# Two transformer blocks on one core: layer parameters loaded in two lots, the first expert step reordered, vector work spread over the recurrence, and squares moved to ScalarE

## What is computed

```python
# block 1 (one layer)
h   = rms_norm(x, norm1_g)                 # w_in: gated linear attention (GLA) + 3 dilated attention groups
gla = gla_chunked(q, k, v, log_a)          # 4 heads of 128, chunks of 16
att = dilated attention, 4 heads, q and k rms-normalised per head of 128
x   = x + (sigmoid gates * (gla proj, att proj)) @ w_out
x   = x + hier_moe(...)                    # 4 groups x 8 experts, width 512, 2 experts per token in one group
# block 2 (two layers l = 0, 1)
z   = rms_norm(x) @ w_in_2[l]              # 2840 columns: spatial gating | RWKV-7 time mix | NSA attention
z_b = z_b + (shift(z_b) - z_b) * mu        # the shift by one token that needs the previous row
rwkv: state = state * w + (state . -kk) (kk * a) + v k, per token, 4 heads of 64
nsa : compressed, selected and windowed attention with rotated queries and keys
x   = x + concat(...) @ w_out_2[l]
x   = x + (l == 0: swiglu, width 2816 | l == 1: 8 experts of width 2816, 2 per token)
x   = x + (p[l] @ ple_proj) * sigmoid(rms_norm(x) @ ple_gate)
```

## Time and profile before

| | |
|---|---|
| runs | 2486.06, 2474.56, 2478.81 us; median 2478.81 |
| profiled execution | 2484.66 us, span of the core 2482.9 us, mean granted TensorE clock 0.963 |
| busy share | PE 94%, PEld 77%, DVE 74%, ACT 59%, POOL 2% |
| DMA | 617.61 MB, mean 249 GB/s |

### The profile page before, as it was taken

The page is one execution under the profiler, slowest core; times in us unless marked ns, Lnnn a source line. Parts: engine busy times, 40 slices in busy tenths (PEclk is TensorE's granted clock), DMA queues, the critical chain, the costliest instruction groups (busy, mean ns, idle before and its releaser), DMA issues.

```text
span 2482.9 us, 30596 instructions
## 1 busy us (share of the span) xinstructions
PE 2335.2 (94%) x12418; PEld 1901.3 (77%) x12418; DVE 1842.8 (74%) x1911; ACT 1469.8 (59%) x1438; POOL 39.1 (2%) x41
## 2 busy tenths in 40 slices
PE   7989988999999998788999998889999999999997
PEld 6878767888888886676788777668888877888885
DVE  5875657888898885676554567578888968888885
ACT  5344536776777774435444553466776756767764
POOL 0000000000000000020000002000000000000000
PEclk8999988999999998899999999889999999999999
DMA  9444445999999995505464551249999988999991
GB/s 234 128 119 136 152 144 206 363 367 355 370 356 370 355 370 168 164 3 178 153 202 165 167 163 53 81 178 364 355 366 359 357 306 301 363 361 358 367 343 52
DMA packets 281225, 617.61 MB, mean 249 GB/s; under 512 B 31848, under 2 KB 130408, under 8 KB 243696
## 3 DMA queue, kind: packets, MB, share of 16 engines
q1 hardware_dynamic: 279664, 611.33, 71.5%
q10 hardware_dynamic: 1408, 4.19, 0.4%
HBM read 612.34 MB, written 1.05 MB: 247 GB/s over the span
## 4 chain that ended last, share of the span: by engine, by line
PE 84%; DVE 9%; ACT 4%; issue 2%; DMA 1%; SPq 0%; DVEq 0%; ACTq 0%
PE ps L566 24%; PE ps L567 24%; PE ps L568 24%; DVE ring_parts L590 3%; ACT high_parts L586 2%; PE ps L2143 1%; PE ps L2782 1%; PE ps L2113 1%; PE ps L3063 1%; PE ps L2114 1%; PE ps L3076 1%; PE ps L2155 0%; PE ps L2154 0%; DMA arena<-arena 0%; DVE arena L1347 0%
## 5 line engine op out<-in xcount | busy, mean ns | idle before, releaser
L590 DVE TENSOR_TENSOR ring_parts<-ring,high_parts 128x2048 fp32r<-128x2048 f32 (+1 forms) x574 | 1282.9, 2274 | 177.4 <-ACT high_parts L586 171.0
L586 ACT CAST high_parts<-ring 128x2048 fp32r<-128x2048 f32 (+1 forms) x574 | 1079.5, 1897 | 194.4 <-PE ps L568 186.8
L568 PE MATMUL ps<-high_parts,arena_parts 128*128 128x512 f32 (+2 forms) x1560 | 621.0, 398 | 0.0
L566 PE MATMUL ps<-high_parts,hT_parts 128*128 128x512 f32 (+2 forms) x1120 | 459.3, 410 | 32.4 <-DVE ring_parts L590 13.7
L567 PE MATMUL ps<-ring_parts,hT_parts 128*128 128x512 f32 (+2 forms) x1120 | 447.8, 400 | 0.0
L566 PE MATMUL ps<-high_parts 128*128 128x512 f32 x912 | 365.2, 400 | 0.0
L567 PE MATMUL ps<-ring_parts,high_parts 128*128 128x512 f32 x912 | 359.3, 394 | 0.0
L568 PE MATMUL ps<-high_parts 128*128 128x512 f32 x912 | 356.5, 391 | 0.0
L568 PEld LDWEIGHTS ps<-high_parts,arena_parts 128*128 128x128 f32 x1560 | 300.6, 193 | 69.2
L566 PE MATMUL ps<-high_parts,arena_parts 128*128 128x512 f32 x744 | 294.9, 396 | 10.5 <-DVE ring_parts L590 4.7
L567 PE MATMUL ps<-ring_parts,arena_parts 128*128 128x512 f32 x744 | 294.1, 395 | 0.0
(11 more groups left out here) (531 smaller groups left out, 1837.8 us busy)
## 6 DMA issues: line engine op xcount, KB each, us to landing
ring<-in_moe_w SPq DMA_DIRECT2D x248, 1024.0 KB, 5.5
ring<-in_w_gate SPq DMA_DIRECT2D x64, 1024.0 KB, 6.0
ring<-in_w_up SPq DMA_DIRECT2D x64, 1024.0 KB, 5.8
ring<-in_w_down SPq DMA_DIRECT2D x64, 1024.0 KB, 5.8
ring<-in_w_in SPq DMA_DIRECT2D x104, 256.0 KB, 4.5
ring<-in_ffn_w SPq DMA_DIRECT2D x44, 512.0 KB, 5.0
ring<-in_w_in SPq DMA_DIRECT2D x20, 1024.0 KB, 5.1
ring<-in_moe_w SPq DMA_DIRECT2D x32, 512.0 KB, 5.0
```

What stands on the lines that cost most here:

```text
L566: pe.matmul(dst, a_hi, b_hi, start=first, stop=False, skip_group_check=True)
L568: return pe.matmul(dst, a_lo, b_hi, start=False, stop=last, skip_group_check=True)
L586: act.copy(high_flat(p), raw_flat(p)).then_inc(upper, 1)
L590: dve.tensor_tensor(raw_flat(p, ring_parts_flat), raw_flat(p), f32(high_flat(p)), ALU.subtract).then_inc(split, 1)
```

## The change

Five edits. (1) `load_layer` becomes `load_soon` (11 loads) and `load_later` (9 loads: the two layer-norm rows, the gating bias and weights, the position and compression weights). In layer 0 pieces 0 to 4 are streamed first, then the 11, pieces 5 to 8, the first shift, pieces 9 on, the second shift, and then the 9. In layer 1 both lots are issued in a row where all 20 stood. PE waits for the second lot after the first scores (slot 20), DVE in hook (10, 0). (2) Expert stages: in step 0 ACT also splits up piece 0 of step 1 and runs the silu ahead of the router's exponential, and DVE takes low parts of step 1's pieces 0 and 1 around the gate weights; in step 1 PE runs up piece 0, then the gates, up piece 1, then turns step 0's hidden part. For b = 4 the gates come after up piece 1 instead of after piece 3. `rows` on DVE comes before piece 1 instead of piece 2. (3) `masked` moves from ahead of level 1 to behind `rw_z1`. (4) Both key rotations at k = 1; the queries' rotation is cut: first product at k = 2, three at k = 3, the two sums in the loop over chunks. (5) ACT makes the dilated squares, right behind its evacuation of the block.

```diff
+        LATER = (8, 9, 10, 14, 15, 16, 17, 18, 19)
@@ SP, layer 0
-                    stream(sp, pieces[0:4])
+                    stream(sp, pieces[0:5])
                     sp.wait_ge(sig("xT_psum"), XT_AT["mix0"] + KC // 2)
-                    load_layer(sp, 0)
-                    stream(sp, pieces[4:10])
+                    load_soon(sp, 0)
+                    stream(sp, pieces[5:9])
...
                 shift_sp(sp, l, 0)
-                stream(sp, pieces[10:])
+                stream(sp, pieces[9:] if l == 0 else pieces[10:])
                 shift_sp(sp, l, 1)
+                if l == 0:
+                    load_later(sp, 0)
@@ first_act hook (phase 1) / dil_squares
+                    if i == 2 * keys_block(h):
+                        after_block(act, keys_block(h))
+                        if h == 0:
+                            act.wait_ge(sig("g_o"), 3)
+                        act.activation(d_sq[h], d_z[h % 2][:, 0:6]..., ACT.Square).then_inc(sig("d_rt"), 1)
-                vstep(dve, dve.tensor_tensor(d_sq[h], qk, qk, ALU.mult))
+                dve.wait_ge(sig("d_rt"), 2 * h + 1)
                 dve.tensor_reduce(d_ss, d_sq[h], AX, ALU.add).then_inc(sig("d_ms"), 1)
@@ moe_main_pe
-                if held:
+                if held and s > 1:
                     turn(held)
...
                 up(st, 0)
+                if s == 1:
+                    pe.wait_ge(*ended(f"{f.name}_gates"))
+                    gates(0)
...
                 up(st, 1)
+                if grouped and b:
+                    gates(b)
+                if s == 1:
+                    turn(held)
                 for h in range(2, len(st.up)):
...
-                if grouped:
-                    pe.wait_ge(*ended(f"{f.name}_gates"))
-                    gates(b)
@@ moe_main_act
+                    if s == 1 and h == 0:
+                        continue
                     split_high(act, p)
-                if st is f.plan[0]:
-                    router_exp_act(act, f)
-                if grouped:
+                    if s == 1 and h == 1:
+                        gate(0)
+                if s == 0:
+                    split_high(act, f.plan[1].up[0])
+                if grouped and b:
                     gate(b)
...
                 silu(st)
+                if s == 0:
+                    router_exp_act(act, f)
@@ moe_main_dve
-                    if grouped and h == 2:
+                    if grouped and h == 1:
                         rows(b)
+                    if s == 1 and h < 2:
+                        continue
...
+                if s == 0:
+                    split_low(dve, f.plan[1].up[0])
                     gates1_dve(dve) if f is moe1 else gates2_dve(dve)
+                    split_low(dve, f.plan[1].up[1])
@@ rwkv, DVE
-                dve.wait_ge(*at("rw_scores", 2))
-                ... six products, then rw_masked
                 for k in range(1, LEV):
                     ... rw_z{k}
+                    if k == 1:
+                        masked()
                     dve.wait_ge(*at(f"rw_dt{k}"))
...
                         ins.then_inc(sig(f"rw_H{n + 1}"), 1)
+                        if n == 0:
+                            dve_aside(dve, "queries")
@@ dve_aside
-                if k in (1, 2): one key rotation each
-                elif k == 3: rotate(dve, n_qr, z[:, :, CQ:CKC], CH)
+                if k == 1: both key rotations
+                elif k in (2, 3):
+                    rotate(dve, n_qr, z[:, :, CQ:CKC], CH, ((0,), (1, 2, 3))[k - 2])
+                elif k == "queries":
+                    rotate(dve, n_qr, z[:, :, CQ:CKC], CH, (4, 5)).then_inc(sig("nsa_rot"), 1)
```

More of the change, by code:

```diff
@@ L828, in layer_loads, with load_soon, load_later, loaded_later @@
             return lot
[L830 to L834, removed]
+        LATER = (8, 9, 10, 14, 15, 16, 17, 18, 19)
+        N_SOON = len(layer_loads(0)) - len(LATER)
+        def load_soon(eng, l):
+            for k, (dst, src) in enumerate(layer_loads(l)):
+                if k not in LATER:
+                    eng.dma_start(dst, src).then_inc(sig("layer_params"), 16)
+        def load_later(eng, l):
+            for k, (dst, src) in enumerate(layer_loads(l)):
+                if k in LATER:
+                    eng.dma_start(dst, src).then_inc(sig("params"), 16)
+        def loaded_later(l):
+            return sig("params"), 16 * (len(P1_LOADS) + len(LATER) * (l + 1))
         MI = Arena(arena)
@@ L1261, in hook @@
                 for h in range(DH):
+                    if i == 2 * keys_block(h):
+                        after_block(act, keys_block(h))
+                        if h == 0:
+                            act.wait_ge(sig("g_o"), 3)
+                        act.activation(d_sq[h], d_z[h % 2][:, 0:6].rearrange("p k t e -> p (k t) e"), ACT.Square)\
+                            .then_inc(sig("d_rt"), 1)
                     if i == D_TURN[h] // 2:
@@ L2188, in moe_main_pe @@
             held = None
-            for st in f.plan:
+            for s, st in enumerate(f.plan):
                 b = st.bucket
-                if held:
+                if held and s > 1:
                     turn(held)
@@ L2344, in moe_main_dve @@
             select(0)
+            assert f.plan[0].n == 512
             held, before = None, None
-            for st in f.plan:
+            for s, st in enumerate(f.plan):
                 b = st.bucket
@@ L2623, in pe_ @@
                     mm.then_inc(sig("rw_scores"), 1)
+                    pe.wait_ge(*loaded_later(l))
                     for h in range(AH):
@@ L2930, in dve_, with masked @@
                 dve.tensor_tensor(w_T, w_T, idn, ALU.add).then_inc(sig("rw_t1"), 1)
-                dve.wait_ge(*at("rw_scores", 2))
-                for k, (dst, m) in enumerate(((w_MT, tri_str_c), (w_RB, tri_inc_c), (w_RK, tri_inc_c))):
-                    for s in range(2):
-                        part = slice(s * NT * HP, (s + 1) * NT * HP)
-                        bank, col = ((1, 2), (1, 2), (3, 0))[k][s], (k % 2) * S
-                        ins = dve.tensor_tensor(dst[:, part, :], blocks(ps[:, bank, col:col + S]), wide(m[:], NT * HP), ALU.mult)
-                ins.then_inc(sig("rw_masked"), 1)
+                def masked():
+                    dve.wait_ge(*at("rw_scores", 2))
+                    for k, (dst, m) in enumerate(((w_MT, tri_str_c), (w_RB, tri_inc_c), (w_RK, tri_inc_c))):
+                        for s in range(2):
+                            part = slice(s * NT * HP, (s + 1) * NT * HP)
+                            bank, col = ((1, 2), (1, 2), (3, 0))[k][s], (k % 2) * S
+                            ins = dve.tensor_tensor(dst[:, part, :], blocks(ps[:, bank, col:col + S]), wide(m[:], NT * HP), ALU.mult)
+                    ins.then_inc(sig("rw_masked"), 1)
                 def bonus(k):
@@ L3273, in act_, with rotate @@
                     act.copy(hT_parts_flat[:, k * 512:(k + 1) * 512], ps[:, ACC + k - 2, :]).then_inc(sig("nsa_out"), 1)
-            def rotate(dve, dst, src, n):
+            def rotate(dve, dst, src, n, steps=range(6)):
                 a = src.rearrange("p t (h n) -> p t h n", n=HD)
@@ L3733, in _ @@
                     sp.wait_ge(*ended("nsa_cmp", 1))
-                    load_layer(sp, 1)
+                    load_soon(sp, 1)
+                    load_later(sp, 1)
                     stream(sp, sorted([p for up in ffn.up for p in up] + ffn.down, key=lambda p: p.n))
```

38 lines of the change are left out of this document (17 added, 21 removed), and 2 rows, old and new, of the table at.

## The result

| | before | after |
|---|---|---|
| median of runs | 2478.26 us (2474.56 to 2486.06, 4 runs) | 2444.61 us (2443.80 to 2448.53, 4 runs) |
| ratio, 95% interval | | 0.9863 [0.9837, 0.9889] |
| second comparison | 2480.07 us (9 runs) | 2444.68 us (5 runs), 0.9854 [0.9831, 0.9877] |
| span of the profiled execution, mean clock | 2482.9 us, 0.963 | 2442.8 us, 0.976 |

The kernel is 34 to 36 us faster; 2441 was forecast, with 2430 to 2459 as the range. The two spans differ by 40.1 us, more than the medians, because the profiled execution of before was a long one, as the prediction said.

The account below looks back on a forecast made before the run. PE was taken to set the pace, transfers close behind, leaving only its idle stretches and the half clock after them to win. Four terms, -15.2 - 20.5 - 1.8 - 0.2 = -37.7 us, gave a median of 2441, range 2430 to 2459.

Parts of the forecast that it names:

- Part 1: Layer 0's input projection: loads in two lots let the first shift land by 985 to 988, PE not waiting; -15.2 us.
- At most 15.3 us are there to win: Layer 0's stretch between first and last block evacuations, 81.3 us, against layer 1's 66.0 for the same work.
- six pieces of 1 MB are 17 us, so it came in behind them: Layer 0's first shift reached DVE 16.7 us after issue because six pieces at 370 GB/s were ahead.
- Part 2: Expert stages: first steps of moe1 -6.4 us and moe2 -7.0, bucket 4's gates -7.1; together -20.5.
- Part 3: Recurrence, both layers: shorter PE waits for `rw_z` less later masks, -0.9 us per layer, -1.8; ends -4.6 and +2 x 2.05.
- Part 4: Attention, squares on ACT: head 0 gains, head 2's wait grows by about 1.5 us; net -0.2, ends -3.5 and +5.6.
- -1.75: Head 0: PE's 4.58 us wait for the norm shortens as DVE loses the 1.76 us square to ACT.
- The sum: Whole kernel: -15.2 - 20.5 - 1.8 - 0.2 = -37.7 us, profiled 2484.66 to 2447.0, median 2441.
- B: Layer 0: shift still lands 16.7 us after issue, bringing only about 5.4 of 15.2 us; 2451, chance 0.14.
- A: Expert stages: transfers limit them, so the start gains are given back; -17.2 remain, 2461.6, chance 0.08.
- C: First two expert steps: new waits replace the old, parts of -13.4 us lost; 2454.5, chance 0.08.
- D: Expert stages: PE granted half clock for longer, slower above 75 us more at half; over 2491 above 100, chance 0.03.

Follow-up runs that it names:

- after_again: The changed kernel run once more with nothing altered, beside the other kernels of that call; 2444.68 us, ratio 0.9854 [0.9831, 0.9877] to the kernel before.
- p2_experts: Kernel before with only the new order of the first expert steps, bucket 4's gates and `rows` one piece earlier; ratio 0.9908 [0.9882, 0.9934].
- p3_recurrence: Kernel before with only the masks moved behind z1 and the key and query rotations spread; ratio 0.9983 [0.9972, 0.9993], 4.2 us.
- p4_squares: Kernel before with only the dilated squares moved to ACT; ratio 1.0001 [0.9991, 1.0010].

## Why the prediction was right, and where it was off

- **Part 1, -15.2: right, -16.9 in the trace and 17 us alone.** The shift was issued right behind the evacuation and the wait fell to 0.28, as forecast. Two things inside it were off. "At most 15.3 us are there to win" took layer 1 as the floor; layer 0 is now at 64.4 us and layer 1 at 66.0, because layer 1 has a half-clock stretch of 3.4 us itself. The 11 loads took SP 6.6 us and not 9.3, which changed nothing, since the shift waited for ACT. And the account "six pieces of 1 MB are 17 us, so it came in behind them" left out that the shift's four copies took SP from 986.98 to 993.3, and that they land 4.4 to 12 us after their issue. The landing, forecast at 985 to 988, came at 989 on before's scale (983.4 + 5.6), only 2 us ahead of DVE. By the same account either half of the edit should have brought nearly all of it; each brought 6.7. The prediction did not price the halves, so the error did not show in its number; that four pieces ahead were few enough was in part luck. The waits for the second lot, priced at 0, do not appear in the trace.
- **Part 2, -20.5: right, -20.4 (6.5, 6.9 and 7.0 against 6.4, 7.0 and 7.1).** The new waits are 0.27, 0.52 and 0.45 us where 0.6 to 0.8 and 0.5 were forecast. The removed and new waits of moe1 differ by 4.0 us, so 2.5 of 6.5 are clock (2.4 forecast). That match is in part luck: in after_again and p2_experts 3.4 us of half clock stay, the gain in moe1 is 5.6 and 5.7, and the three gains add to 19.6. The product of step 1 came at 27.9 and 27.3 us after the first up piece in place of 26.8 and 26.1: DVE's low parts, not PE, set it there. One step later the whole gain is in. In moe2 a wait of 1.11 us for a low part is new.
- **Part 3, -1.8: right in sign, within half a us by its waits; timed alone it came out larger.** The waits for `rw_z` fell from 4.6 to 1.9 where I had 4.6 - 2.5 = 2.1, and the masks' wait is 1.3 where I had 0.6; by waits it is -1.4 in the changed kernel and, with masks' waits of 0.4 and 0.2, -2.2 in p3_recurrence. The lower end of the timed 4.2 us [1.7, 7] holds this. The masks carry nearly nothing of it. The query product that took 1.24 us beside POOL's mask takes 0.29 at its new level; at the next one two products take 1.44 us (DVE at 1061.86, POOL's mask at 1061.51), so the blocked time moved one level on, as the prediction had it.
- **Part 4, -0.2: the net is right, and within what the runs can tell (1.0001 alone); one of its two terms holds in one case only.** In the profiled execution 4.58 became 2.79 (2.8 forecast) and 2.84 became 4.20 (4.4 forecast). ACT's square took 1.47 us (1.4 forecast), without a table load ahead of it. "-1.75" took 4.58 as the wait of this code; where PE comes later, it was 1.42 before and 0.6 to 0.7 after, and the term is -0.7 to -0.8. Taking back head 2 alone won 5.1 us, of which the wait of the sum explains 1.4.
- **The sum, -37.7**: by the stretches of the traces 16.9 + 20.4 and 1.4 us of waits in the recurrences make 38.7, the span fell by 40.1, and the medians by 33.7 and 35.4. The measured 2444.61 lies 3.6 us above the forecast 2441.
- **The rivals.** B (the shift lands 16.7 us after issue whatever is ahead) is out: 7 us from the first issue (976.27) to the landing. A is out by the windows at x90 and by SP's 1827.8 us of waits for PE. C is out by the waits of half a us. D is out: no half clock in the stages' middle, and 117 us at half in the whole profiled execution (0.024 x 2443 / 0.5), 184 before. A second execution of the changed kernel had a mean clock of 0.970, 147 us.

## What to carry to other kernels

A small copy that an engine waits for is late by everything that its queue has issued before it and the DMA engines have not worked off: count SP's issue time, the bytes ahead, the copy's own landing, and the small packets of parameter loads, and move all of them until the copy is early; half of the move wins half of the wait and nothing of the clock. Price a wait of TensorE with the half-clock work that follows it, here 2.5 us beside 4.0 us of waits in moe1's first steps and 4.1 beside 12.7 in layer 0, but take it as a range: it differed between executions of the same code. In layer 0 halving the wait gave none of it back, removing the wait gave all. Before a difference of clock is called the effect of an edit, look at the same stretch in every trace that has the same code there. When work is given to another engine, do it per instance: in heads 0, 1 and 3 ACT was free, in head 2 DVE needed something queued behind it.

## What the runs showed of the hardware

- **A wait's cost in clock has little to do with its length.** Over the 20 us around the wait at 210 us the clock was 0.91 in three traces and 0.83 in one with a wait of 4.2 us, 0.91 in eight and 1.00 in two with one of 2.84. In layer 0 waits of 6.3 and 13.0 us both cost 4.1 us of clock, one of 14.3 (p4_squares, stretch 80.1 us) 1.7.
- **Half clock ahead of a wait shortens the wait.** The first attention turn waited 4.6 us with PE's 15 us of work ahead of it at full clock and 1.4 with a mean clock of 0.77 there, the same code in both.
- **The same code runs with its half-clock stretches in other places.** Two executions of the changed kernel had mean clocks of 0.976 and 0.970 and spans 2442.8 and 2445.4. PE in p4_squares was 0.6 us ahead of before at moe1's first up piece (384.21 against 384.80) and 5.0 us ahead at moe2's last product (2420.46 against 2425.44), over stages in which no instruction differs. A difference below some 5 us between two traces is read from waits, not from offsets.
- **A 2 KB copy from SBUF to SBUF took 10.8 to 12.0 us behind ring pieces still on their way, 4.4 us when they were nearly through, and 1.7 us with none ahead.** It landed 2.1 to 3.5 us behind the last of them.
